# Hybrid attention trunk on one core: inverse norms of the queries as a row scale, head sums on column strips, memory keys and values in one product

## The chip, the cores and the metric

The kernel runs on one core of a Trainium2 chip. The metric is the device time of one execution in microseconds (us). Engines go by short names: PE is the matrix engine (TensorE), PEld its weight loads, DVE the vector engine, ACT the scalar engine, POOL the GpSimd engine, SP the engine that issues the weight loads from memory. A matmul here takes a stationary operand (K partitions by M columns) and streams N columns past it. A bank is one of PE's eight result buffers (128 partitions by 512 fp32 columns).

## The reference, cut to what matters

Two layers; 512 tokens, width 1024. The two SwiGLU parts and the output product are the same in both kernels. What the change touches is the mixing part between them:

```python
h = rms_norm(x, mix_norm[l]); z = h @ w_in[l]
aq, ak, av, iq, ik, iw, pu, mq = jnp.split(z, IN_OFFSETS, axis=-1)
aq = rms_norm(aq.reshape(B, S, 8, 64), q_norm[l])      # per head: a / rms(a) * gain
ak = rms_norm(ak.reshape(B, S, 8, 64), k_norm[l])
y_attn = dsa_attention(aq, ak, av, iq, ik, iw)         # top 128 keys by an indexer, softmax(q.k / 8) v
y_pool = multiscale_pool(pu, w_pool[l], pool_scale[l])
mk, mv = split(rms_norm(mem, mem_norm[l]) @ w_mem_kv[l])   # 256 memory tokens, 4 heads x 64
y_mem = softmax(rms_norm(mq) . rms_norm(mk) / 8) mv
x = x + concat(y_attn, y_pool, y_mem) @ w_out[l]
```

A row of logits is a query's dot products with all keys. 1/rms of the query is one number for the whole row, and the gain of the query can as well be multiplied into the keys.

## The kernel before, in words

Everything is written out by hand: each engine has its own program, and semaphores (`wait_ge`, `then_inc`) order them. A layer is `ffn`, `mix`, `ffn`. Activations lie transposed, channels on partitions, tokens on columns, as tiles of 128x512. Every fp32 product is made of three passes on rounded halves (hi.hi, hi.lo, lo.hi), so one product of a 128x128 weight block with a tile is three matmuls of 512 columns.

**Weights** come as a stream of slots of 512 KB (8 blocks of 128x128) through a ring of four. For a slot, SP loads `raw`; ACT (`round_ahead`, L911) waits until PE has finished the slot four places back, writes the rounded `w_hi` and the negated `w_lo`; POOL (`rest`, L380 on) issues a DMA that adds `raw` into `w_lo`; then PE may start the slot. In `mix` the slots are, in this order, iq 2, ik, iw, av 4, aq 4, ak 4, mq 2, pu 2, mk 2, mv 2, out 8.

**mix, projections.** `project_z` (L660) multiplies one slot with all of h into bank t % 4: 24 matmuls of 512 columns. DVE multiplies it by 1/rms of the tokens (`evacuate`, L1184) into a tile z, ACT squares it (`squares`, L1000) into one of two buffers, and PE sums the squares of each head (`heads_sum`, L584): one unrounded fp32 matmul a tile, 20 columns of selector against 512 tokens, all accumulated on rows 0 to 19 of bank 6. After the tenth tile ACT takes the root, DVE the reciprocal (`head_inverse`), and two small steps split it in hi and lo. Between the evacuations DVE takes the top eight scores of each token over and over (`take_largest`, L1228): 16 rounds a layer.

**mix, spreads and memory.** PE brings each head's inverse rms back to the head's 64 channel rows (`spread_rms`, L690: two matmuls with K = 20 into a bank), for all 4 query tiles, 4 key tiles, 2 memory query tiles and 2 memory key tiles, in `NORM_ORDER`; DVE multiplies the tile by it and the gain (`normalise`), ACT rounds it (`split_hi`), POOL makes the rest (L434). Between the spreads PE makes the memory keys (slots mk, 256 columns a matmul, channels on partitions) and the memory values (slots mv, tokens on partitions, 256 columns). Eight spreads stand ahead of the first logits, four behind.

**mix, attention.** 48 units: query tile 3 first, of each tile 8 heads and 4 memory heads. PE makes logits of two units at a time on the two row halves (`logits`, L781) in three banks in turn; DVE adds the mask, scales by -1/8 and takes the row's maximum (`mask_and_max`, L1310 on); ACT the exponential; PE transposes it (L806), DVE or ACT copies it, PE multiplies with the values on the two column halves (`times_v`, L810). Then the output product.

Of the kernel before, what the change touches and what calls it, by code (L numbers as in the profile page):

```python
# [21 lines left out]
P = 128  # L22
D = 1024
T = 512
LAYERS = 2
HD = 64
# [17 lines left out]
MIX_SLOTS = (("iq", 2), ("ik", 1), ("iw", 1), ("av", 4), ("aq", 4), ("ak", 4), ("mq", 2), ("pu", 2),  # L44
             ("mk", 2), ("mv", 2), ("out", 8))
# [12 lines left out]
G_Q, G_K, G_MQ, G_MK, G_POOL = (4 * DC + i for i in range(5))  # L58
# [3 lines left out]
ZT = HEADS // 2 * 2 + MEM_HEADS // 2  # L62
NORMED = ZT + MEM_HEADS // 2

Z_ROWS = 2 * ZT
MK_ROW = 32
MK_ROWS = 2 * (NORMED - ZT)
NROW = MK_ROW + MK_ROWS
# [4 lines left out]
C_SEL_MK = C_SEL + ZT * Z_ROWS  # L73
C_INV = C_SEL_MK + (NORMED - ZT) * MK_ROWS
# [8 lines left out]
ROUNDS_AT = (1, 1, 1, 1, 1, 1, 2, 2, 2, 2)  # L83
FIRST_ROUNDS = ROUNDS - sum(ROUNDS_AT)
# [14 lines left out]
ORDER = [0, 1, 2, 3, 4, 5, 6, 7, 8, 9, "mk"]  # L99

NORM_ORDER = [0, 4, 1, 5, 2, 6, 3, 7, 8, 9, 10, 11]
NORM_EARLY = 8

POOL_CHAIN = 14
ROUND_CHAIN = 2 * (TT - 1)
DVE_CHAIN = 104


def build(nc, x_t, mem_t, weights, pool_w, params, consts, spreads, out):
# [13 lines left out]
    def new(name, cols, dt=f32, parts=P):  # L123
# [4 lines left out]
    x = new("x", DC * T)  # L128
    h_hi = new("h_hi", DC * T, f32r)
# [16 lines left out]
    spread = new("spread", NORMED * P, f32r, NROW)  # L146
# [9 lines left out]
    wb = place("wb", T, a_lo_at + 11 * tile_b)  # L156
# [5 lines left out]
    hrms = place("hrms", T, a_lo_at, parts=NROW)  # L162
    hr_hi, hr_lo = (a_lo[0:NROW, i * T:(i + 1) * T] for i in (6, 7))
    spread_in = place("spread_in", NORMED * P, a_hi_at + 4 * tile_b, parts=NROW)
    v = place("v", TT * T, a_lo_at + 12 * tile_b)
    mk = place("mk", 2 * MEM, a_lo_at + 16 * tile_b)
    mv = place("mv", MT * MEM, a_lo_at + 17 * tile_b)
# [3 lines left out]
    rmem = place("rmem", MEM, small)  # L171
    negmax, rowsum, rinv = (
        place(name, UNITS, small + (MEM + i * UNITS) * 4)
        for i, name in enumerate(("negmax", "rowsum", "rinv")))
    top8 = place("top8", 8 * TT, small + (MEM + 3 * UNITS) * 4)
    sq = place("sq", DC * T, a_lo_at + 14 * tile_b)

    zn_hi = [h_hi[:, j * T:(j + 1) * T] for j in range(8)] + \
            [a_hi[:, j * T:(j + 1) * T] for j in (8, 9)] + \
            [a_hi[:, 10 * T + i * MEM:10 * T + (i + 1) * MEM] for i in range(2)]  # L180
    zn_lo = [h_lo[:, j * T:(j + 1) * T] for j in range(8)] + \
            [a_lo[:, j * T:(j + 1) * T] for j in (8, 9)] + \
            [a_lo[:, 10 * T + i * MEM:10 * T + (i + 1) * MEM] for i in range(2)]

    pt = [place(f"pt{i}", T, a_hi_at + (12 + j) * tile_b) for i, j in enumerate((0, 4, 6, 7))]

    prob = [t1[:, 0:T], t1[:, T:2 * T]] + \
           [place(f"prob{j}", T, a_hi_at + (12 + j) * tile_b)[:, :] for j in (1, 5)]


    rt = place("rt", T, a_hi_at + (12 + 2) * tile_b)
    yt = place("yt", T, a_hi_at + (12 + 3) * tile_b)
# [51 lines left out]
    mcols_done = sem("mcols_done")  # L244
    mcols_ready = sem("mcols_ready")
    v_ready = sem("v_ready")
    mv_ready = sem("mv_ready")
# [10 lines left out]
    spread_loaded = sem("spread_loaded")  # L258
# [49 lines left out]
    def spread_bank(k):  # L308

        return bank[k % 3 if k < NORM_EARLY else (7, 6)[k % 2]]  # L310

# [27 lines left out]
    def head_rms(j):  # L339

        return (slice(0, Z_ROWS), T) if j < ZT else (slice(MK_ROW, NROW), MEM)

    with nc.Block() as block:
# [32 lines left out]
        def _(pool):  # L376
# [15 lines left out]

            def pooling(l):

                wait_apart(pool, proj_ready, l * 17 + 16)
                for i in range(2):
                    ui = chunk(u, i)

# [25 lines left out]
            with pool.Fori(0, LAYERS) as l:  # L424
                with pool.Fori(0, ahead // RING) as i:
                    for pos in range(RING):
                        rest(l, (i * RING, pos))
# [1061 lines left out]
```

## Time and profile before

| | |
|---|---|
| median of 3 runs | 1983.04 us |
| lowest | 1982.92 us |
| the profiled execution, first to last instruction | 1981.4 us |
| PE busy | 1948.7 us (98%) |
| granted PE clock, mean | 0.996 of 2.4 GHz |
| sum of all waits of PE matmuls that the profile puts down to another engine or a DMA | 29.0 us |

The profile has no run time for the profiled execution other than its span; the median of the runs lies 1.6 us above it. Times in the trace count from the start of the span. The mixing part of the first layer runs from about 377 to 639 us, that of the second 979.8 us later. A busy PE is not one at its peak: the start of each matmul to the start of the next tells what it costs, since their ends overlap.

### The profile page before, as it was taken

The page shows a single profiled execution, that of the slowest core. Times are in us where ns is not written, and L with a number is a line of the kernel's source. Part 1 is how long each engine was busy: PE and PEld are TensorE (multiplying, and loading weights), DVE is VectorE, ACT ScalarE, POOL GpSimd, SP SyncE. Part 2 cuts the span into 40 slices and gives each one's busy share as a digit, 9 for nine tenths or more (in the row PEclk, how much of TensorE's full clock was granted, in tenths as well). Part 3 has the DMA queues.
Part 4 walks back from the last instruction along what each step waited for, and adds up shares of the span by engine and source line. Part 5 has one row for each costly group of instructions (what it writes and reads, how often), then busy time and mean ns, then how long its engine had stood idle before and what let it go on. Part 6 is the DMA issues. An engine that isn't in the chain of part 4 may idle for free.

```text
span 1981.4 us, 27709 instructions
## 1 busy us (share of the span) xinstructions
PE 1948.7 (98%) x9256; PEld 1571.9 (79%) x9256; DVE 617.1 (31%) x1180; ACT 1086.5 (55%) x1393; POOL 350.7 (18%) x404
## 2 busy tenths in 40 slices
PE   6999999999999999999999999999999999999999
PEld 4888888886768888888878888888767688888887
DVE  3222200367662322220052222004676532222101
ACT  6655543563584655553375565336546666565432
POOL 1111111111431111111111111111116111111111
PEclk9999999999999999999999999999999999999999
DMA  7988888887336888888878888888762379888886
GB/s 217 218 188 192 195 190 194 190 192 176 83 87 144 195 188 190 193 194 194 195 170 200 189 186 199 196 195 200 185 155 54 87 170 206 194 197 189 195 195 180
DMA packets 97799, 354.54 MB, mean 179 GB/s; under 512 B 11000, under 2 KB 11256, under 8 KB 97472
## 3 DMA queue, kind: packets, MB, share of 16 engines
q0 software_dynamic: 47232, 171.99, 48.7%
q1 hardware_dynamic: 49824, 178.84, 27.5%
q10 hardware_dynamic: 672, 2.80, 0.4%
q8 instruction: 40, 0.66, 0.1%
q14 instruction: 31, 0.25, 0.1%
HBM read 179.52 MB, written 2.10 MB: 92 GB/s over the span
## 4 chain that ended last, share of the span: by engine, by line
PE 97%; DMA 1%; ACT 1%; issue 1%; DVE 0%; SPq 0%; DVEq 0%; ACTq 0%; POOLq 0%
PE bank L453 95%; PE bank L806 2%; DMA w_lo<-raw 1%; DMA x<-x_t 0%; ACT w_lo L920 0%; ACT prob L1066 0%; DVE pt L336 0%; ACT a_hi L1082 0%; ACT t L1066 0%; DVE t L1323 0%; DVE x L1150 0%; DVE z L1277 0%; ACT pt L1059 0%; ACT mv L1046 0%; DVE yt L1341 0%
## 5 line engine op out<-in xcount | busy, mean ns | idle before, releaser
L919 ACT ACTIVATE w_hi<-raw 128x1024 fp32r<-128x1024 f32 x329 | 349.0, 1061 | 645.5 <-PE bank L453 630.8
L453 PE MATMUL bank<-h_hi,w_hi 128*128 128x512 f32 x1664 | 654.6, 393 | 15.9 <-ACT h_hi L891 13.9
L453 PE MATMUL bank<-h_hi,w_lo 128*128 128x512 f32 x1664 | 649.5, 390 | 5.6 <-DMA w_lo<-raw 5.6
L453 PE MATMUL bank<-h_lo,w_hi 128*128 128x512 f32 x1664 | 632.9, 389 | 0.0
L385 POOL DMA_DIRECT2D w_lo<-raw x328 | 283.5, 866 | 1589.6 <-ACT w_lo L920 1549.7
L453 PEld LDWEIGHTS bank<-h_hi,w_hi 128*128 128x128 f32 x1664 | 313.3, 188 | 97.5 <-ACT h_hi L891 15.3
L453 PEld LDWEIGHTS bank<-h_hi,w_lo 128*128 128x128 f32 x1664 | 313.3, 188 | 71.3 <-DMA w_lo<-raw 6.1
L453 PEld LDWEIGHTS bank<-h_lo,w_hi 128*128 128x128 f32 x1664 | 312.4, 188 | 65.5 <-issue 1.2
L920 ACT ACTIVATE w_lo<-raw 128x1024 fp32r<-128x1024 f32 x329 | 343.5, 1044 | 0.0
L453 PE MATMUL bank<-a_hi,w_hi 128*128 (+2 forms) x864 | 334.1, 387 | 0.0
L453 PE MATMUL bank<-a_lo,w_hi 128*128 (+2 forms) x864 | 332.8, 385 | 0.0
L453 PE MATMUL bank<-a_hi,w_lo 128*128 (+2 forms) x864 | 332.7, 385 | 0.0
L1150 DVE SCALAR_TENSOR_TENSOR x<-bank,x 128x512 f32<-128x512 f32 x48 | 32.7, 692 | 512.8 <-PE bank L453 512.8
L453 PEld LDWEIGHTS bank<-a_hi,w_hi 128*128 128x128 f32 x864 | 162.2, 188 | 35.0 <-issue 2.8
L453 PEld LDWEIGHTS bank<-a_hi,w_lo 128*128 128x128 f32 x864 | 162.3, 188 | 32.7
L453 PEld LDWEIGHTS bank<-a_lo,w_hi 128*128 128x128 f32 x864 | 162.3, 188 | 32.0
L1168 DVE TENSOR_TENSOR t<-bank,r 128x512 f32<-128x512 f32 x88 | 60.8, 691 | 384.2 <-PE bank L453 384.2
L919 ACT ACT_TABLE_LOAD x45 | 57.7, 1283 | 129.0 <-PE bank L453 121.1
L1165 DVE TENSOR_TENSOR t<-bank,r 128x512 f32<-128x512 f32 x88 | 60.9, 692 | 165.3 <-PE bank L453 163.6
L1174 DVE TENSOR_TENSOR a_lo<-t,a_hi 128x512 f32 x88 | 61.0, 693 | 107.8 <-ACT a_hi L938 107.8
L1172 DVE TENSOR_TENSOR t<-t,t 128x512 f32<-128x512 f32 x88 | 60.9, 692 | 11.1 <-ACT t L935 0.8
L935 ACT ACT_TABLE_LOAD x44 | 56.5, 1283 | 0.8
(138 smaller groups left out, 1273.9 us busy)
## 6 DMA issues: line engine op xcount, KB each, us to landing
raw<-weights SPq DMA_DIRECT2D x332, 512.0 KB, 4.6
w_lo<-raw POOLq DMA_DIRECT2D x328, 512.0 KB, 5.7
x<-x_t SPq DMA_DIRECT2D x4, 512.0 KB, 7.3
mem<-mem_t ACTq DMA_DIRECT2D x2, 1024.0 KB, 7.1
out_t<-x SPq DMA_DIRECT2D x8, 256.0 KB, 2.1
const<-consts SPq DMA_DIRECT2D x1, 505.5 KB, 10.1
spread_in<-spreads ACTq DMA_DIRECT2D x2, 216.0 KB
wpool<-pool_w ACTq DMA_DIRECT2D x2, 128.0 KB, 7.0
```

The lines of the kernel that those rows point to most:

```text
L385: G.dma_start(w_lo[:, s], raw[:, s], accum_op=ALU.add).then_inc(w_ready[pos], 16)
L453: return nc.tensor.matmul(out_, lhsT, rhs, start=start, stop=stop, skip_group_check=True)
L806: last = nc.tensor.transpose(bank[2 + n % 2][:, b * P:(b + 1) * P], prob[n % 4][:, b * P:(b + 1) * P], con(C_ID, P))
L919: nc.scalar.activation(w_hi[:, s], raw[:, s], ACT.Copy).then_inc(w_hi_done, 1)
L920: nc.scalar.activation(w_lo[:, s], raw[:, s], ACT.Copy, scale=-1.0)\
L935: nc.scalar.activation(g, g, ACT.Silu).then_inc(silu_ready, 1)
L1150: V.scalar_tensor_tensor(out=chunk(x, j), in0=bank[j][:, :], scalar=scale, in1=chunk(x, j), op0=ALU.mult, op1=ALU.add)\
L1165: V.tensor_tensor(out=g, in0=bank[2 * half][:, :], in1=r[:, :], op=ALU.mult).then_inc(gate_ready, 1)
L1168: V.tensor_tensor(out=h, in0=bank[2 * half + 1][:, :], in1=r[:, :], op=ALU.mult).then_inc(gu_free, 1)
L1172: V.tensor_tensor(out=h, in0=g, in1=h, op=ALU.mult).then_inc(prod_ready, 1)
L1174: V.tensor_tensor(out=a_lo[:, ds(f * T + half * T, T)], in0=h, in1=a_hi[:, ds(f * T + half * T, T)].bitcast(f32), op=ALU.subtract).then_in ...
```

## The change

1. **Queries.** Query tiles are no longer normalised. They are split in hi and lo as soon as they are evacuated (hi on ACT behind `square`, lo on POOL between the weight steps). The product of both gains, `gain_qk`, goes on the keys. The roots of the queries' sums are transposed by PE (`root_columns`), so that tokens lie on partitions, DVE inverts them with the factor -1/8 into `rq`, and `mask_and_max` takes `rq`'s column as its scale where it had a constant.
2. **Head sums.** `heads_sum(g)` handles four tiles in one group: four fp32 matmuls with 32 columns of selector each, whose results lie on the four 32-row strips of bank 6. Three groups (queries, keys, memory queries) take the place of ten sums of tiles.
3. **Key spreads.** Heads' inverse rms of the four key tiles lie on four 32-row strips; eight matmuls with K = 32 (four tiles, hi and lo) into banks 4 to 7 stand in one group. No other spreads are left.
4. **Memory keys and values.** One product with tokens on partitions: 4 slots kv, 48 matmuls of 512 columns, moved between ak and mq. ACT scales both by 1/rms of the memory tokens, DVE makes the heads' sums, inverses and normalised keys with tokens on partitions, PE transposes them (4 transposes).
5. The rounds of `take_largest` are dealt out anew (2 first, 10 between the tiles, 4 late), the tiles of the attention part move to the place of h, and the matrix of spreads is no longer loaded from memory.

```diff
-MIX_SLOTS = (("iq", 2), ("ik", 1), ("iw", 1), ("av", 4), ("aq", 4), ("ak", 4), ("mq", 2), ("pu", 2),
-             ("mk", 2), ("mv", 2), ("out", 8))
+MIX_SLOTS = (("iq", 2), ("ik", 1), ("iw", 1), ("av", 4), ("aq", 4), ("ak", 4), ("kv", 4), ("mq", 2),
+             ("pu", 2), ("out", 8))
-ROUNDS_AT = (1, 1, 1, 1, 1, 1, 2, 2, 2, 2)
-FIRST_ROUNDS = ROUNDS - sum(ROUNDS_AT)
+ROUNDS_AT = (1, 2, 1, 1, 1, 2, 1, 1)
+LATE_ROUNDS = 4
+FIRST_ROUNDS = ROUNDS - sum(ROUNDS_AT) - LATE_ROUNDS
...
@@ PE
-                def heads_sum(j):
-                    pe.wait_ge(zsq_ready, l * (ZT + 1) + (j + 1))
...
-                        last = mm(bank[6][0:Z_ROWS, :], con(C_SEL + ORDER[j] * Z_ROWS, Z_ROWS),
-                                  chunk(t1, j % 2), j == 0, j == ZT - 1)
+                def heads_sum(g):
+                    pe.wait_ge(zsq_ready, l * ZT + (QT, 2 * QT, ZT)[g])
...
+                    for s in range(QT):
+                        last = mm(bank[6][s * STRIP:(s + 1) * STRIP, :], con(C_SEL, STRIP),
+                                  squares[s % MQT if g == 2 else s])
                     last.then_inc(zsum_done, 1)
+                def root_columns(g):
+                    pe.wait_ge(hrms_ready, l * ROOT_GROUPS + (g + 1))
+                    if g == 2:
+                        pe.wait_ge(zn_ready, (l + 1) * QT)
+                    for i in range(TT):
+                        last = nc.tensor.transpose(bank[7][:, i * P:(i + 1) * P],
+                                                   hrms[g][:, i * P:(i + 1) * P], con(C_ID, P))
+                    last.then_inc(rq_done, 1)
...
+                def project_kv(s):
+                    n = at("kv", s)
+                    lo_ready_of(l, n)
+                    for half in range(2):
+                        k = 2 * s + half
+                        for i in range(MT):
+                            last = passes(bank[4 + i][:, :], pair(m_hi, m_lo, k * MEM + i * P, P),
+                                          weight(n % RING, half * T, T), k == 0, k == DC - 1)
+                    last.then_inc(slot_done, 1)
                 for i in range(4):
                     project_z(4 + i, "aq", i)
...
+                project_z(8, "ak", 0)
+                heads_sum(0)
+                project_z(9, "ak", 1)
+                project_z(10, "ak", 2)
+                root_columns(0)
+                project_z(11, "ak", 3)
+                pe.wait_ge(m_lo_ready, l + 1)
+                project_kv(0)
+                project_kv(1)
+                heads_sum(1)
+                project_kv(2)
+                project_kv(3)
                 project_z(12, "mq", 0)
+                pe.wait_ge(spread_ready, l + 1)
+                pe.wait_ge(hr_lo_ready, l + 1)
+                pe.wait_ge(kv_ready, (l + 1) * MT)
...
+                for part, hr in enumerate((hr_hi, hr_lo)):
+                    for s in range(QT):
+                        rows = slice(s * STRIP, (s + 1) * STRIP)
+                        last = mm(bank[4 + s][:, :], spread[rows, :], hr[rows, :], part == 0, part == 1)
...
                 project_z(13, "mq", 1)
+                pe.wait_ge(mk_n_ready, l + 1)
+                pe.wait_ge(zn_ready, l * QT + 1)
+                for c in range(MQT):
+                    for i in range(MT):
+                        last = nc.tensor.transpose(bank[4][:, c * MEM + i * P:c * MEM + (i + 1) * P],
+                                                   mk_n[:, i * MEM + c * P:i * MEM + (c + 1) * P],
+                                                   con(C_ID, P))
+                last.then_inc(mkt_done, 1)
                 project_z(14, "pu", 0)
+                heads_sum(2)
                 project_z(15, "pu", 1)
+                root_columns(2)
...
@@ ACT
+                for j in range(QT):
                     round_ahead(l, MIX_BASE["aq"] + j)
+                    square(j)
+                    split_hi(j)
+                for j in range(QT):
+                    round_ahead(l, MIX_BASE["ak"] + j)
+                    if j == 0:
+                        head_root(0)
+                    square(QT + j)
+                round_ahead(l, MIX_BASE["kv"])
+                round_ahead(l, MIX_BASE["kv"] + 1)
                 head_root(1)
+                round_ahead(l, MIX_BASE["kv"] + 2)
+                act.wait_ge(hinv_ready, l + 1)
+                nc.scalar.activation(hr_hi, hrms[1][:, :], ACT.Copy).then_inc(hr_hi_ready, 1)
+                round_ahead(l, MIX_BASE["kv"] + 3)
+                act.wait_ge(rmem_ready, l + 1)
                 for i in range(MT):
+                    nc.scalar.activation(chunk(kv, i), bank[4 + i][:, :], ACT.Copy,
+                                         scale=rmem_col[:, i:i + 1]).then_inc(kv_ready, 1)
...
@@ DVE, from the eighth tile on
+                for j in range(2 * QT):
+                    evacuate_z(j)
+                    rounds(ROUNDS_AT[j])
+                inverse_columns(0)
+                dve.wait_ge(hrms_ready, l * ROOT_GROUPS + 2)
+                V.reciprocal(hrms[1][:, :], hrms[1][:, :]).then_inc(hinv_ready, 1)
+                rounds(1)
+                dve.wait_ge(hr_hi_ready, l + 1)
+                V.tensor_tensor(out=hr_lo, in0=hrms[1][:, :], in1=hr_hi.bitcast(f32),
+                                op=ALU.subtract).then_inc(hr_lo_ready, 1)
+                dve.wait_ge(kv_ready, (l + 1) * MT)
...
+                V.tensor_reduce(mk_rms[:, :], mk_sq[:, :].rearrange("p (g d) -> p g d", d=HD),
+                                mybir.AxisListType.X, ALU.add).then_inc(mk_sum_ready, 1)
+                rounds(1)
+                evacuate_z(2 * QT)
...
-                                           scale=-HD ** -0.5, scalar=-TAKEN, op0=ALU.add, op1=ALU.min,
+                                           scale=unit_rq(n), scalar=-TAKEN, op0=ALU.add, op1=ALU.min,
```

On PE, behind the last projection of the kernel before (slot pu 1): a spread's matmul reads `a_lo` (where the inverse rms lie) and `spread`; matmuls on `a_hi`/`a_lo` with `w_` of 256 columns are the memory keys.

```order
L453 MATMUL bank<-h_hi,w_lo 128x512
L696 REGISTER_ALU
L698 REGISTER_ALU
L453 MATMUL bank<-a_lo,spread 128x512 x2
...
L453 MATMUL bank<-a_hi,w_hi 128x256
L453 MATMUL bank<-a_lo,w_hi 128x256
L453 MATMUL bank<-a_hi,w_lo 128x256
```

The same engine in the changed kernel, behind the slot mq 0 and behind the slot mq 1:

```order
L472 MATMUL bank<-h_hi,w_lo 128x512
L728 REGISTER_ALU
L730 REGISTER_ALU
L472 MATMUL bank<-a_hi,spread 128x512 x8
L695 REGISTER_ALU
...
L741 ISA
L744 MATMUL bank<-const,mk_n 128x128 x4
```

All spreads stand in one piece now, with a projection behind it, and the memory keys reach PE again only as four transposes, behind one more projection.

On DVE, ahead of the first mask of the kernel before (names: `score` is the mask, `hrms` the inverse rms of the heads):

```order
L1277 SCALAR_TENSOR_TENSOR z<-z,par,bank 128x512 x4
L1290 REGISTER_ALU
L1293 TENSOR_TENSOR mk<-bank,rmem 128x256 x2
L1277 SCALAR_TENSOR_TENSOR z<-z,par,bank 128x512 x3
L1261 REGISTER_ALU
L1262 RECIPROCAL hrms<-hrms 4x256
L1267 TENSOR_TENSOR a_lo<-hrms,a_lo 4x256
L320 ISA
L1323 ISA t_59,negmax<-bank,score 128x512
```

On DVE in the changed kernel, from the split of the keys' inverse rms to the normalised memory keys:

```order
L1299 TENSOR_TENSOR a_hi<-hrms_k,a_hi 128x512
L1303 REGISTER_ALU
L1305 TENSOR_TENSOR mk_sq<-kv 128x512
L1139 REGISTER_ALU
L1307 TENSOR_REDUCE mk_rms<-mk_sq 128x8
...
L1206 TENSOR_TENSOR z<-bank,r 128x512
L1313 ISA
L1315 SCALAR_TENSOR_TENSOR z<-z,gain_qk,bank 128x512
...
L1318 RECIPROCAL mk_rms<-mk_rms 128x8
L1139 REGISTER_ALU
L1321 TENSOR_TENSOR mk_n<-kv,mk_rms 128x256 x2
```

Between the reduction and the evacuation of `z` stands one round of `take_largest` (three MAX, three MATCH_REPLACE). The twelve multiplications of tiles by spread inverses have become four, and a chain of memory keys stands among them.

## Rows read from the trace of the kernel before

**Rows 1.** The page, busy time of each engine.

```profile
PE 1948.7 (98%) x9256; PEld 1571.9 (79%) x9256; DVE 617.1 (31%) x1180; ACT 1086.5 (55%) x1393; POOL 350.7 (18%) x404
```

**Rows 2.** PE, timeline, projections of the first layer (start us, us, engine, line, operation, idle before).

```profile
404.69 0.39 PE L453 MATMUL bank<-w_hi,h_hi 128*128 128x512 f32 x1
...
415.35 0.39 PE L453 MATMUL bank<-w_hi,h_lo 128*128 128x512 f32 x1
...
477.70 0.50 PE L453 MATMUL bank<-h_hi,w_hi 128*128 128x512 f32 x1
...
483.37 1.03 PE L453 MATMUL bank<-t,const 128*20 128x512 f32 x2
484.34 0.60 PE L453 MATMUL bank<-const,rmem 1*128 1x1 f32 x4
...
503.82 1.89 PE L453 MATMUL bank<-t,const 128*20 128x512 f32 x4
```

**Rows 3.** PE, timeline, spreads and memory products, first layer.

```profile
511.47 1.18 PE L453 MATMUL bank<-a_lo,spread 20*128 20x512 f32 x4
...
512.80 0.28 PE L453 MATMUL bank<-a_lo,w_hi 128*128 128x256 f32 x1
...
515.43 0.28 PE L453 MATMUL bank<-a_hi,w_lo 128*128 128x256 f32 x1
...
529.15 0.50 PE L453 MATMUL bank<-h_hi 64*128 64x512 f32 x2
```

**Rows 4.** The chain that ended last (start us, us, what), second layer and first.

```profile
1491.31 17.76 PE bank L453 x116
549.03 0.59 PE bank L806 x4
```

**Rows 5.** PE, timeline, unrounded products with the values on column halves.

```profile
540.98 1.09 PE L453 MATMUL bank<-pt,v 128*64 128x128 f32 x16
542.01 0.39 PE L453 MATMUL bank<-a_hi 64*128 64x256 f32 x2
```

**Rows 6.** PE, timeline, the first logits.

```profile
531.77 0.50 PE L453 MATMUL bank<-h_hi 64*128 64x512 f32 x2 [0.54 <-DVE negmax L1323]
532.11 0.40 PE L453 MATMUL bank<-h_lo,h_hi 64*128 64x512 f32 x2
532.34 0.39 PE L453 MATMUL bank<-h_hi,h_lo 64*128 64x512 f32 x2
...
534.42 0.79 PE L453 MATMUL bank<-h_hi 64*128 64x512 f32 x2
```

**Rows 7.** Stretches of the attention's start: us, busy of each engine, granted clock, DMA share, GB/s.

```profile
534.00:540.00 6.00, 6.00 (x25) 3.96 (x25) 4.01 (x12) 4.45 (x12) 5.79 (x10) 0.50 0.01 1
```

**Rows 8.** DVE, timeline, a round of the top eight, a reciprocal, the first mask.

```profile
497.90 1.47 DVE L1236 MAX8 top<-score 128x8 f32<-128x512 f32 x3
...
500.86 1.47 DVE L1236 MAX8 top<-score 128x8 f32<-128x512 f32 x3
...
506.61 3.34 DVE L1262 RECIPROCAL hrms<-hrms 20x512 f32<-20x512 f32 x1 [1.99 <-ACT hrms L1018]
...
531.02 0.69 DVE L1323 CUSTOM_DVE_ANT_0 t<-bank,score 128x512 f32<-128x512 f32 x1
```

**Rows 9.** ACT, timeline, rounding of one slot.

```profile
504.00 1.06 ACT L919 ACTIVATE w_hi<-raw 128x1024 fp32r<-128x1024 f32 x1 [4.18 <-PE bank L453]
504.97 1.04 ACT L920 ACTIVATE w_lo<-raw 128x1024 fp32r<-128x1024 f32 x1
```

**Rows 10.** The page, DMA queues and issues (KB each, us to landing).

```profile
q0 software_dynamic: 47232, 171.99, 48.7%
q1 hardware_dynamic: 49824, 178.84, 27.5%
...
raw<-weights SPq DMA_DIRECT2D x332, 512.0 KB, 4.6
w_lo<-raw POOLq DMA_DIRECT2D x328, 512.0 KB, 5.7
```

More of the change, by code:

```diff
@@ L57 @@
 G_FFN1, G_MIX, G_FFN2, G_MEM = 0, DC, 2 * DC, 3 * DC
-G_Q, G_K, G_MQ, G_MK, G_POOL = (4 * DC + i for i in range(5))
+G_Q, G_MQ, G_K, G_MK, G_POOL = (4 * DC + i for i in range(5))
 PARAMS = 4 * DC + 4 + 2
[L62 to L68, printed above, removed]
+QT = HEADS // 2
+MQT = MEM_HEADS // 2
+ZT = 2 * QT + MQT
+STRIP = 32
+PROJ = 3 + 1 + ZT + 2
+ROOT_GROUPS = 3
 C_ID = 0
@@ new lines, in mix @@
+                square(2 * QT)
+                for j in range(QT, 2 * QT):
+                    act.wait_ge(zn_ready, l * QT + (j - QT + 1))
+                    act.wait_ge(zlo_ready, l * ZT + (j - QT + 1))
+                    split_hi(j)
+                square(2 * QT + 1)
+                split_hi(2 * QT)
+                split_hi(2 * QT + 1)
+                act.wait_ge(mkt_done, l + 1)
+                act.wait_ge(gain_ready, l + 1)
+                nc.scalar.activation(zmk_hi, bank[4][:, :], ACT.Copy,
+                                     scale=gain_qk[:, 1:2]).then_inc(mk_hi_ready, 1)
@@ L1252, in mix, with rounds @@
+                def rounds(n):
+                    for _ in range(n):
                         take_largest(l * DVE_CHAIN + links[0])
                         links[0] += ROUND_CHAIN
[L1254 to L1262 removed]
@@ new lines, in mix @@
+                evacuate_z(2 * QT)
+                dve.wait_ge(gain_ready, l + 1)
+                for s in range(QT):
+                    dve.wait_ge(spread_done, l * QT + (s + 1))
+                    t = chunk(z, QT + s)
+                    V.scalar_tensor_tensor(out=t, in0=t, scalar=gain_qk[:, 0:1], in1=bank[4 + s][:, :],
+                                           op0=ALU.mult, op1=ALU.mult).then_inc(zn_ready, 1)
+                dve.wait_ge(mk_rms_ready, l + 1)
+                link(l, V.reciprocal(mk_rms[:, :], mk_rms[:, :]))
@@ new lines, in mix @@
+                for i in range(MT):
+                    s = slice(i * MEM_HEADS, (i + 1) * MEM_HEADS)
+                    last = V.tensor_tensor(
+                        out=mk_n[:, i * MEM:(i + 1) * MEM].rearrange("p (h d) -> p h d", d=HD),
+                        in0=kv[:, i * T:i * T + MEM].rearrange("p (h d) -> p h d", d=HD),
+                        in1=mk_rms[:, s].unsqueeze(2).broadcast_to([P, MEM_HEADS, HD]), op=ALU.mult)
+                last.then_inc(mk_n_ready, 1)
+                rounds(1)
@@ L1402, in _constants @@
     c[:, C_EPS] = EPS
-    return c
-def _spread():
-    import numpy as np
-    c = np.zeros((NROW, NORMED * P), np.float32)
-    for head in range(2 * NORMED):
-        row = head if head < Z_ROWS else MK_ROW + head - Z_ROWS
-        c[row, head * HD:(head + 1) * HD] = 1
     return c
```

364 lines of the change are left out of this document (142 added, 222 removed).

## The prediction

> **What bounds the kernel now.** I read the page first: PE is busy for 1948.7 us of a span of 1981.4 [rows 1], so a change pays what it takes from PE's own stream and from the few places where PE stands. Since the ends of matmuls overlap, I price them by the distance between starts, in the timeline of PE. The unrounded sums and the spreads stand in the mixing part alone, so I read one layer's and count it twice: the last piece ahead of the attention is 17.76 us long in the second layer [rows 4], as from 511.47 to 529.15 in the first [rows 3].
>
> Prices of one step: 48 matmuls of 512 columns in sequence start 10.66 us apart, first to last, so 0.227 us each [rows 2]. A projection with a head sum behind it takes 6.64 us (477.70 to 484.34), and 24 x 0.227 is 5.45: a sum costs 1.20. Two sums at once show 1.89 against 1.03 us: the second adds 0.86. So 0.86 is the unrounded matmul of 512 columns itself, and 0.34 the change of shape there and back [rows 2]. Of 256 columns, 23 matmuls start 2.63 us apart, first to last, 0.120 each [rows 3]: two of them cost 0.24, where one of 512 columns costs 0.227. Four transposes cost 0.59 [rows 4].
>
> Rows 6 and 7 show where PE stands: between the first logits (529.15) and the third pair (534.42) it waits for DVE's masks and spreads, and the granted clock is 0.50, which is 1.2 GHz, from 534 to 540.
>
> **What the change removes, for one layer.** Ten head sums: eight alone and one pair, 8 x 1.20 + 2.06 = 11.7 us. The columns of the memory's rms: 0.5 (start of the row to the next projection) [rows 2]. The whole piece from 511.47 to 529.15 with eight spreads, memory keys, memory values and the keys' sum: 17.7 [rows 3]. Together 29.9. Twelve projections of tiles stay. The mean square of the memory stays one short step.
>
> **What it adds, for one layer.** Memory keys and values: 48 x 0.227 = 10.9. Two transpositions of the roots and one of the memory keys: 3 x (0.59 + 0.2 for the change of shape, of which 0 to 0.34 is possible) = 2.4.
>
> The three groups of sums are the disputed term. If the four strips run at the same time, a group costs what one sum does, 1.2. If they run in pairs, 2 x 0.86 + 0.34 = 2.1. If they run one behind the other, 4 x 0.86 + 0.34 = 3.8. No row shows four strips. Two column halves do run together: eight unrounded products of 128 columns should take 8 x 0.86/4 = 1.7 us one by one, and take 1.03 with the change of shape [rows 5]. That is so close to full overlap that I take 1.4 for a group of four, just above full overlap and below pairs; three groups are 4.2, between 3.6 and 11.4. The Trainium skill, TensorE: Matmul & The Clock Gate, section Measured speedup vs the span model, gives 2.38 times for three column strips and 3.07 times for four row strips; an estimate by 3.07 is 4 x 0.86/3.07 + 0.34 = 1.46 a group, 4.4 for three, which would move the forecast by 0.4 us. No run here shows it yet.
>
> Spreads: eight rounded matmuls with K = 32 on four row strips. Two row halves overlap fully: the pair at 532.11 is followed by the next 0.23 us later, which is the price of one matmul [rows 6]. All four at once would be 2 x 0.227 + 0.34 = 0.8, one by one 8 x 0.227 + 0.34 = 2.1; I take 0.9.
>
> **Waits.** With T for the end of the fourth key projection, PE runs kv 0 and 1 (5.5), a group of sums (1.4), kv 2 and 3 (5.5), mq 0 (5.5), and reaches the spreads at T+17.9 and the memory keys' transposes at T+24.2. The chain on ACT and DVE: ACT roots the keys' sums at T+8.4, behind rounding a slot (1.9 us a slot, [rows 9]); DVE's reciprocal takes 3.34 [rows 8], so T+11.8; ACT rounds the first half of it, then waits in `round_ahead(kv 3)` for the raw slot. That load may start only when the slot's `w_lo` has landed: T + 2.3 for ACT + 5.7 + 4.6 [rows 10] = T+12.6, some 2 us later if the short slots crowd the queues. So ACT scales kv by T+15.8 to T+17.5: no wait at the spreads. Queued behind that on DVE are square and reduction (1.6 with the wait between), one round of the top eight (2.96, [rows 8]), the evacuation of mq 0 (0.69, as the mask's row of 512 columns), four key tiles (2.8), and memory keys (1.1): T+25 to T+26.7 against T+24.2. PE waits there 0.9 to 2.6 us; I take 1.8, with 0 to 3.5 as bounds. Behind PE's wait stand pu 0, the last sums and pu 1, and nothing else is late for them. Ahead of the first logits PE now waits for the evacuation of pu 1, partly under the transposes: 0.3.
>
> The sum added is 10.9 + 2.4 + 4.2 + 0.9 + 1.8 + 0.3 = 20.5, and 29.9 - 20.5 = 9.4 saved.
>
> **The weight stream.** A kv slot keeps PE for 12 x 0.227 = 2.7 us where others keep it 5.4. A slot is ready 2.3 (ACT) + 5.7 (landing) = 8.0 us after the slot four places back is done. For kv 3 three short slots and a sum stand between, 9.6 us: slack 1.6. For mq 0 it is alike. Before, the four memory slots were drawn out over 17.7 us. In engine time a slot costs 0.487 x 1981/328 = 2.9 us for the addition and 0.275 x 1981/332 = 1.6 for the load [rows 10], 4.6 against 2.7. I take no wait, with up to 3 us a layer as the far bound.
>
> **The start of the attention.** The 5.27 us from the first to the third pair hold four spreads, four multiplications on DVE and the late memory inverse: the first mask starts at 531.02, about 0.9 us after its logits, since DVE was splitting it [rows 8]. Without these, a pair of logits takes 0.8 to 0.9, the mask may start 0.25 behind, and the pairs come 2.0 us apart: 4.1, which saves 1.2 (0 to 2). ACT and POOL shed four tiles each there. The half clock stays: PE still stands about 1.1 us twice, as much as before. The scale of the mask read from memory instead of a constant I cost at nothing: the row's 0.69 us for 512 columns is one column per step, with the mask read beside it. ACT's earlier splits (0.6 each, four) lie in its waits for PE, 4 us a slot [rows 9]; POOL's lie between its slots. If it cost 0.1 us more, the three pairs at the start would carry 0.2 each, 0.6 a layer.
>
> So a layer saves 9.4 + 1.2 = 10.6 us, both 21.2; the profiled span would be 1960.2, and the median, 1.6 above, 1961.8.
>
> **The rivals.**
> - **PE keeps its full clock** at the attention's start. The six microseconds from 534 to 540 are all busy at half clock [rows 7], so up to 3.0 is lost; with it back, 2 x 3.0 less: 1955.8. For it: the spreads that waited are gone. Against it: PE still stands for masks. The rule of the Trainium skill (TensorE: Matmul & The Clock Gate, section HAM oscillation) asks for long idle gaps before a fall; the gap here was 0.54 us [rows 6], twice, so the trace does not bear it out, and I keep the fall.
> - **Strips do not overlap.** Groups 3.8, spreads 2.1: 7.2 + 1.2 = 8.4 more a layer, 1978.6. Against it speaks [rows 5].
> - **Slower than before: each strip pays the change of shape.** If PE drains between strips, a strip's sum costs the 1.20 of a sum of today, twelve of them 14.4 instead of 4.2, and eight spreads 8 x 0.57 = 4.5 instead of 0.9: 13.8 more a layer, 1989.4. It turns slower once a group of sums costs over 1.4 + 10.6/3 = 4.9 us. Against it: eight products on halves in 1.03 us [rows 5] leave no room for a drain between them.
> - **The weights come late.** The short slots crowd the queues, PE stands 3 us for kv 3 or mq 0, and the clock falls once more (3.0): 6.0 a layer, 1973.8. It decides from a landing over 7.3 us.
>
> **How the numbers follow.** The forecast holds 0.70, with a range of its own of 1955 to 1969: waits 0 to 3.5 instead of 1.8 (-4 to +3), groups 1.2 to 2.1 (-1 to +4), the start 0 to 2 (-2 to +2). Full clock 0.12, late weights 0.08, strips in sequence 0.07, drains 0.03. The range of 1951 to 1975 leaves out the two last and edges of the others. A change of 2% is about what a measurement of this kernel can tell from no change: faster than 1943.4 needs a saving of 20 us a layer, which only the full clock together with every lower bound comes near, 0.02; slower than 2022.7 is 0.01; the rest 0.97.
>
> **What would show it.** Each group of sums adds 1.2 to 1.6 us between two projections, the eight spreads under 1.0; the piece from the memory's mean square to the first logits is 9 to 10 us shorter; PE stands at the transposes of `mk_n` for a release by DVE; the first three pairs of logits stand 2 us apart; the clock is half for some 6 us behind them. I am wrong if a wait for `w_lo` shows inside kv, if a group takes over 2.1, or if the attention itself, from the third pair to the output product, changes its length by more than 2 us, since I let nothing of it count.

## The result and the profile after

| | before | after |
|---|---|---|
| median | 1982.98 us (4 runs) | 1968.45 us (4 runs) |
| the profiled execution | 1981.4 us | 1965.5 us |
| PE matmuls | 9256 | 9148 |
| PE busy | 1948.7 us | 1918.9 us |

One of the four runs before took 2177.24 us, far slower than the three others, and is left out of the ratio. The ratio of the times is 0.993, with a 95% interval of 0.9918 to 0.9942: faster by 0.7%, well within the 2% that count as no change. The forecast was 1961.8 us, its range 1951 to 1975.

The page of the changed kernel, busy time, then the issues (the lines that answer to [rows 1, 10]):

```profile
PE 1918.9 (98%) x9148; PEld 1559.4 (79%) x9148; DVE 614.1 (31%) x1176; ACT 1082.7 (55%) x1391; POOL 347.6 (18%) x400
...
raw<-weights SPq DMA_DIRECT2D x332, 512.0 KB, 4.7
w_lo<-raw POOLq DMA_DIRECT2D x328, 512.0 KB, 5.8
```

PE shed 29.8 us of busy time, yet the span only 15.9. The other half must stand somewhere as idle time. PE's waits in the changed kernel (what it waited for: us in total, times, longest):

```profile
PE bank L744 <- DVE mk_n L1321: 8.5, 2, 4.3
PE bank L472 <- DMA w_lo<-raw: 7.7, 2, 5.7
PE bank L472 <- DVE negmax L1364: 4.3, 4, 1.1
...
PE bank L472 <- ACT kv L1049: 1.5, 1, 1.5
```

The line of `mk_n` is new and the largest wait that the change brought: twice 4.3 us at the transposes of the memory keys. PE's timeline there and at the spreads, first layer (start, us, engine, line, operation, idle before):

```profile
497.88 0.74 PE L472 MATMUL bank<-a_hi,spread 32*128 32x512 f32 x8 [1.53 <-ACT kv L1049]
498.55 0.50 PE L472 MATMUL bank<-h_hi,w_hi 128*128 128x512 f32 x1
...
508.55 0.65 PE L744 MATMUL bank<-const,mk_n 128*128 128x128 f32 x4 [4.26 <-DVE mk_n L1321]
508.96 0.61 PE L472 MATMUL bank<-h_hi,w_hi 128*128 128x512 f32 x1
...
512.34 0.50 PE L472 MATMUL bank<-h_hi,w_lo 128*128 128x512 f32 x1
```

From 508.96 to 512.34 eight matmuls take 3.38 us where they take 1.8 elsewhere (8 x 0.227). The stretches say why: behind the wait the clock is granted at half. Stretches of both places (us, busy of each engine, granted clock, DMA share, GB/s):

```profile
509.00:510.00 1.00, 1.00 (x5) 0.81 (x4) 1.00 (x5) 0.00 (x0) 0.55 (x1) 0.58 0.00 0
510.00:511.00 1.00, 1.00 (x3) 0.79 (x3) 1.00 (x5) 0.00 (x0) 0.00 (x0) 0.50 0.00 0
...
525.00:533.00 8.00, 5.98 (x52) 4.10 (x52) 7.00 (x20) 6.49 (x17) 7.34 (x10) 1.00 0.01 3
```

At the start of the attention, where [rows 7] had half clock, it now stays full (last line).

The chain that ended last, which here led through PE before [rows 4], now leaves it. Read it downwards: each piece was released by the one above (start, us, what):

```profile
479.81 1.05 ACT w_lo L932
...
481.42 6.17 DMA w_lo<-raw
487.75 6.48 DMA raw<-weights
...
494.59 1.06 ACT w_hi L931
...
496.60 1.16 ACT kv L1049 x2
497.78 0.70 DVE mk_sq L1305
...
502.75 2.63 DVE z L1315 x4
...
506.94 1.49 DVE mk_n L1321
508.55 0.65 PE bank L744 x4
```

So the memory keys wait for a weight load that they don't use: ACT stands in `round_ahead` for the raw slot of pu 1 (landed at 494.2) and only then scales kv. Behind that comes DVE's queue.

The head sums, first layer, and the two parts of kv around the second group:

```profile
460.72 1.06 PE L472 MATMUL bank<-t,const 128*32 128x512 f32 x8
461.72 0.50 PE L472 MATMUL bank<-h_hi,w_hi 128*128 128x512 f32 x1
...
478.64 0.39 PE L472 MATMUL bank<-w_hi,a_hi 128*128 128x512 f32 x1
...
484.17 1.06 PE L472 MATMUL bank<-t,const 128*32 128x512 f32 x8
485.17 0.50 PE L472 MATMUL bank<-w_hi,a_hi 128*128 128x512 f32 x1
...
490.75 0.39 PE L472 MATMUL bank<-h_hi,w_hi 128*128 128x512 f32 x1
```

A group of four sums costs 1.2 with the change of shape, what one sum cost before [rows 2]. The 24 matmuls from 478.64 take 5.5, as priced.

The first logits, which answer to [rows 6]: three pairs 2.0 us apart, 523.80 to 527.88, 4.08 us in place of 5.27, with a wait of 1.1 for a mask ahead of the second and of the third.

```profile
523.80 0.72 PE L472 MATMUL bank<-a_hi 64*128 64x512 f32 x4 [0.43 <-DVE u L1206]
...
525.85 0.73 PE L472 MATMUL bank<-a_hi 64*128 64x512 f32 x4 [1.09 <-DVE negmax L1364]
...
527.88 0.73 PE L472 MATMUL bank<-a_hi 64*128 64x512 f32 x4 [1.07 <-DVE negmax L1364]
...
531.91 1.09 PE L472 MATMUL bank<-pt,v 128*64 128x128 f32 x16
```

**The ledger**, by marks that both kernels have (us, before and after):

| stretch of the mixing part | layer 1 | saved | layer 2 | saved |
|---|---|---|---|---|
| first index logits to first logits | 101.67 / 96.67 | 5.00 | 101.67 / 96.02 | 5.65 |
| first logits to first product with the values | 11.83 / 8.11 | 3.72 | 11.72 / 8.11 | 3.61 |
| from there to the last product with memory values | 57.06 / 57.42 | -0.36 | 57.07 / 57.41 | -0.34 |
| sum | | 8.36 | | 8.92 |

With 0.35 us that it was ahead already at the first mark, and 1.7 that it loses at the start of the second layer, these are the 15.9 us. That loss goes with a fall of the clock behind the wait for the first weights of the second layer (0.81, 0.50 and 0.83 in the three stretches of 2 us from 996). The kernel before has the same wait of 2.0 us there, and no fall.

### The profile page after: what moved, and what is told of

Same layout as the page of the kernel before. It is cut to its first block, busy times and chain, and to the rows that moved or that the text cites. A ratio compares the mean times of both kernels' runs of the same rounds, so it can differ in the third digit from the quotient of the medians.

```text
span 1965.5 us, 27449 instructions
## 1 busy us (share of the span) xinstructions
PE 1918.9 (98%) x9148; PEld 1559.4 (79%) x9148; DVE 614.1 (31%) x1176; ACT 1082.7 (55%) x1391; POOL 347.6 (18%) x400
## 4 chain that ended last, share of the span: by engine, by line
PE 94%; DMA 2%; DVE 1%; issue 1%; ACT 1%; DVEq 0%; SPq 0%; ACTq 0%; POOLq 0%
PE bank L472 92%; PE bank L821 1%; DMA w_lo<-raw 1%; DMA raw<-weights 1%; ACT w_lo L932 0%; DMA x<-x_t 0%; DVE z L1315 0%; DVE mk_n L1321 0%; ACT prob L1086 0%; DVE t L1364 0%; ACT kv L1049 0%; ACT t L1086 0%; ACT w_hi L931 0%; DVE pt L344 0%; PE bank L744 0%
## 5 line engine op out<-in xcount | busy, mean ns | idle before, releaser
L472 PE MATMUL bank<-h_hi,w_hi 128*128 128x512 f32 x1664 | 656.0, 394 | 15.6 <-ACT h_hi L903 13.6
L472 PE MATMUL bank<-a_hi,w_hi 128*128 (+1 forms) x832 | 324.6, 390 | 0.0
L472 PE MATMUL bank<-a_lo,w_hi 128*128 (+1 forms) x832 | 323.8, 389 | 0.0
L472 PE MATMUL bank<-a_hi,w_lo 128*128 (+1 forms) x832 | 323.7, 389 | 0.0
L472 PEld LDWEIGHTS bank<-a_hi,w_hi 128*128 128x128 f32 x832 | 156.2, 188 | 33.7 <-issue 1.4
L472 PEld LDWEIGHTS bank<-a_hi,w_lo 128*128 128x128 f32 x832 | 156.2, 188 | 32.5
L472 PEld LDWEIGHTS bank<-a_lo,w_hi 128*128 128x128 f32 x832 | 156.2, 188 | 32.0
```

Source lines behind the costliest of these rows:

```text
L472: return nc.tensor.matmul(out_, lhsT, rhs, start=start, stop=stop, skip_group_check=True)
```

## The experiments

**1 to 3. The wait at the memory keys.** Two causes stood to be told apart: ACT scales kv late, behind the load for pu 1; and DVE comes to `mk_n` late, behind four key tiles, where its two multiplications ran 1.44 us each. The changed kernel's DVE and POOL there show that they ran at the same time as POOL's subtractions:

```profile
504.24 5.31 POOL L440 TENSOR_TENSOR a_hi<-z,a_hi 128x512 fp32r<-128x512 f32 x4 [6.21 <-ACT a_hi L1019]
...
505.53 2.88 DVE L1321 TENSOR_TENSOR mk_n<-kv,mk_rms 128x256 f32<-128x256 f32 x2
```

`kv_first`: ACT scales kv ahead of rounding the slot of pu 1.

```diff
-                round_ahead(l, MIX_BASE["kv"] + 3)
+                act.wait_ge(slot_done, l * SLOTS + (RING + MIX_BASE["kv"] + 4))
                 act.wait_ge(rmem_ready, l + 1)
                 for i in range(MT):
                     nc.scalar.activation(chunk(kv, i), ...).then_inc(kv_ready, 1)
+                round_ahead(l, MIX_BASE["kv"] + 3)
```

> The changed kernel with one swap on ACT: the memory keys and values are scaled before the slot pu 1 is rounded, so that they no longer stand behind its raw load. Theory 1 (the late load starts the DVE chain late): kv is ready at about 492 instead of 497.8 us, the 1.5 us wait at the spreads goes, the wait at the transposes of mk_n falls from 4.3 to about 2.1 us a layer; some 3 us a layer less, about 1962 us. Theory 2 (DVE's own queue, with the rounds of the top eight, sets when mk_n is ready): the wait stays at 4.3 us and the time at 1968 us.

Measured: 1960.34 us, ratio 0.9885 (0.9869 to 0.9902), span 1958.3. The wait at the spreads is gone, that at `mk_n` falls from 8.5 to 2.8 in two. The two multiplications start at 502.88 and still take 2.97 together.

`mkn_early`: DVE makes the memory keys ahead of the evacuation of mq 0 and of the four key tiles.

```diff
+                dve.wait_ge(mk_rms_ready, l + 1)
+                link(l, V.reciprocal(mk_rms[:, :], mk_rms[:, :]))
...
+                last.then_inc(mk_n_ready, 1)
                 evacuate_z(2 * QT)
                 dve.wait_ge(gain_ready, l + 1)
                 for s in range(QT):
...
-                dve.wait_ge(mk_rms_ready, l + 1)
-                link(l, V.reciprocal(mk_rms[:, :], mk_rms[:, :]))
...
-                last.then_inc(mk_n_ready, 1)
```

> The changed kernel with the reciprocal and the two multiplications of mk_n on DVE moved ahead of the evacuation of mq 0 and the four key tiles; everything else as it is. They then run while POOL does nothing. Theory 1 (each took 1.44 us because POOL's subtractions ran beside them): each takes 0.42 to 0.5 us, PE's wait of 4.3 us at the transposes falls to 0 to 0.5, the half clock behind it goes as well: 4 to 6 us a layer less, about 1957 us. Theory 2 (the operand that is spread over 64 columns costs it): each still takes about 1.4 us, wherever it stands; the wait falls only to 1.5 to 2.5 us, about 1962 us.

Measured: 1959.09 us, ratio 0.9879 (0.9862 to 0.9895), span 1957.2. No wait at `mk_n` is left, and the two multiplications take 0.76 together, with POOL idle until 505.56 but for a DMA issue:

```profile
502.71 0.76 DVE L1314 TENSOR_TENSOR mk_n<-kv,mk_rms 128x256 f32<-128x256 f32 x2
```

So the same instruction starts every 0.4 us alone and 1.4 us beside POOL's subtractions. The wait for kv at the spreads stays (2.6 in two, 2.3 of it in the first layer, where the clock falls behind it: 0.79 from 496 to 504).

`both`: the two edits together.

> Both moves together. If the 4.3 us and the 1.5 us are the late load and the place of mk_n, no wait at the spreads or at the transposes is left, the clock stays full through the projections, and the time is 1952 to 1956 us. If the clock falls by itself (at the attention's start instead, as in the kernel before), 3 us a layer come back and the time is near 1960 us.

Measured: 1954.8 us, ratio 0.9873 (0.9852 to 0.9895), span 1952.7. Neither wait is left, 10.0 us of idle time less. Each edit alone takes away most of the wait at `mk_n` or all of it, so what they gain doesn't add up: 7.2 and 8.3 us of span alone, 12.8 together. Of the 12.8, 10.0 are these waits; the rest goes with the clock, whose falls behind the wait at `mk_n` are gone, while one at the attention's start has come. The clock is full through the first layer's mixing part, but falls at the second layer's start, and at the attention's start in that layer:

```profile
518.00:524.00 6.00, 4.68 (x33) 3.11 (x34) 4.98 (x16) 5.17 (x14) 5.60 (x8) 1.00 0.02 4
1484.00:1492.00 8.00, 6.95 (x34) 4.51 (x32) 5.00 (x16) 4.92 (x14) 7.41 (x10) 0.57 0.01 3
```

**4 and 5. Do the strips overlap?** A group at 1.2 us says so, but a low price of each strip would look alike. `twice` (on the changed kernel) issues every group of sums and the spreads twice over; `one_strip` (on `both`) adds four sums to each group as well, all four on the first strip. Both add matmuls whose results are overwritten.

The added lines of `twice` (the first of them for the sums), then of `one_strip`:

```diff
+                    for s in range(QT):
+                        mm(bank[6][s * STRIP:(s + 1) * STRIP, :], con(C_SEL, STRIP), squares[...])
...
+                for part, hr in enumerate((hr_hi, hr_lo)):
+                    for s in range(QT):
+                        mm(bank[4 + s][:, :], spread[rows, :], hr[rows, :], part == 0, part == 1)
```

```diff
+                    for s in range(QT):
+                        mm(bank[6][0:STRIP, :], con(C_SEL, STRIP), squares[...])
```

> The changed kernel with each group of four head sums and the group of eight spreads issued twice; the second issue overwrites the first with the same values. Theory 1 (four strips run at the same time): a second group of sums adds 0.86 us, a second group of spreads 0.45 us: 3.0 us a layer. Rival (strips in pairs): 1.7 and 0.9 us. Rival (one by one): 3.4 and 1.8 us, 12 us a layer.

> Both moves, and ahead of each group of four head sums four more sums, all on the first strip; the group then overwrites them. Theory 1 (what made the second group cost 0.86 us is that its strips differ): four on one strip run one by one, 3.4 us a group, 10.3 us a layer. Rival (a narrow sum is cheap by itself, whatever strip it takes): 0.9 us a group as in the doubled kernel.

The first group in `twice`, with its spreads, then in `one_strip`:

```profile
460.38 1.92 PE L472 MATMUL bank<-t,const 128*32 128x512 f32 x16
...
500.29 1.22 PE L472 MATMUL bank<-a_hi,spread 32*128 32x512 f32 x16 [2.27 <-ACT kv L1056]
```

```profile
459.96 4.48 PE L472 MATMUL bank<-t,const 128*32 128x512 f32 x16
```

Measured, one run each: 1972.95 and 1973.14 us. Four more sums on four strips add 0.86 us (1.92 for 1.06), the price of a single unrounded matmul of 512 columns; four more on one strip add 3.42, four times that. The eight extra spreads add 0.48 (1.22 for 0.74), which is two matmuls' time for eight. No run puts all eight on one row strip, but the kernel before has spreads on one strip, six and then four in a row, all on the first 20 rows:

```profile
515.64 1.65 PE L453 MATMUL bank<-a_lo,spread 20*128 20x512 f32 x6
...
520.29 1.19 PE L453 MATMUL bank<-a_lo,spread 20*128 20x512 f32 x4
```

There two matmuls more add 0.46, so few rows alone don't make them cheap. Strips overlap fully, column strips as row strips.

**6. The scale from memory.** The prediction let the row's own scale cost nothing. In the changed kernel a mask takes 0.75 us, in [rows 8] 0.69. `const_scale` puts the constant back, on `both`; it leaves out the queries' inverse rms.

```diff
-                                           scale=unit_rq(n), scalar=-TAKEN, ...
+                                           scale=-HD ** -0.5, scalar=-TAKEN, ...
```

> Both moves, and the mask on DVE scales by the constant -1/8 as in the kernel before; the queries' norm is left out of the result. Theory 1 (the scale read per row costs the mask 0.06 us of 512 columns, and that is what the attention lost between the first product with the values and the output product, 0.35 us a layer): masks at 0.69 instead of 0.75 us, the stretch shorter by 0.3 to 0.4 us a layer, the time about 1954 us. Theory 2 (the mask is hidden): masks shorter, the stretch as long as before.

Measured: 1952.27 us, ratio 0.9842 (0.9822 to 0.9862), span 1949.9. The masks of DVE in `both`, then in `const_scale`:

```profile
517.26 0.75 DVE L1363 CUSTOM_DVE_ANT_0 t<-bank,score,rq 128x512 f32<-128x512 f32 x1 [1.29 <-PE bank L472]
```

```profile
516.84 0.69 DVE L1363 CUSTOM_DVE_ANT_0 t<-bank,score 128x512 f32<-128x512 f32 x1 [1.29 <-PE bank L472]
```

0.06 us a mask, and at the attention's start, where PE stands for masks, the three pairs come 1.98 apart instead of 2.05. From the first product with the values to the last with memory values the first layer takes 57.20 instead of 57.44. So the scale costs some 0.1 at the start and 0.24 behind it, a part of the ledger's third line. The rest of its 2.8 us of span is mostly the clock, which did not fall at the attention's start in the second layer here (1.00 from 1481 to 1489); that the shorter mask did that is not shown, since it stays full in the next run too, with the mask at 0.75. The intervals of `both` and of this run overlap.

**7. Wide or narrow.** How much of the gain is the width of kv's matmuls? `narrow_kv` takes `both` and makes kv of 96 matmuls of 256 columns. The two column halves of a bank are accumulated in turns, which changes what memory keys and values hold; its time stands for the matmuls alone.

```diff
-                            last = passes(bank[4 + i][:, :], pair(...), weight(n % RING, half * T, T), ...)
+                            for c in range(0, T, MEM):
+                                last = passes(bank[4 + i][:, c:c + MEM], pair(...),
+                                              weight(n % RING, half * T + c, MEM), ...)
```

> Both moves, and the memory product in 96 matmuls of 256 columns instead of 48 of 512, with the same slots and place. Theory 1 (a matmul of 256 columns starts every 0.120 us, one of 512 every 0.227): the four slots take 11.5 instead of 10.9 us of matmuls, 0.6 us a layer more. Rival (the gain of one product is the saved weight loads, hidden only at 512 columns): 2 us a layer or more.

PE's timeline, the first matmuls of kv and the first behind it:

```profile
479.93 0.28 PE L472 MATMUL bank<-w_hi,a_hi 128*128 128x256 f32 x1
480.05 0.28 PE L472 MATMUL bank<-w_lo,a_hi 128*128 128x256 f32 x1
...
492.63 0.40 PE L472 MATMUL bank<-h_hi,w_hi 128*128 128x512 f32 x1
```

Measured, one run: 1955.9 us. From 479.93 to 492.63 are 12.70 us for kv with a group of sums, where the changed kernel takes 12.11 (478.64 to 490.75). The width is worth 0.6 us a layer, 0.24 against 0.227 for 512 columns as priced. It is no large part of the gain.

**8 and 9. The gaps at the first logits.** In `both` PE still stands 1.1 us for each of two masks, in both layers. `pu_in_gaps` fills them: the last pool projection is cut in two, and a half stands behind the first pair of logits and one behind the second (`root_columns(2)` goes with the first half).

```diff
-                project_z(15, "pu", 1)
-                root_columns(2)
...
                     if n < UNITS:
                         logits(n)
+                    if n < 4:
+                        project_pu1(n // 2)
```

> Both moves, and the last projection (pu 1) cut in two halves of 12 matmuls, one behind the first pair of logits and one behind the second; its evacuation on DVE stands behind the fourth mask, and ACT's third exponential waits for it. Theory 1 (PE's three waits at the attention's start, 0.4 + 1.1 + 1.1 us, are free room): 2.6 us a layer less than both moves alone, and no half clock at that place: 1947 to 1951 us. Theory 2 (the exponential and the mask that now wait set the start anew): the waits come back behind the third pair, the time stays at 1953 to 1956 us.

Measured: 1954.02 us, ratio 0.9853 (0.9834 to 0.9872), span 1951.6. The gaps are filled (0.7 us for masks in two waits, 4.3 before), but PE now stands once a layer ahead of the first logits. Its wait, then the stretch behind it in the first layer:

```profile
PE bank L472 <- DVE u L1222: 3.8, 2, 1.9
```

```profile
510.00:516.00 6.00, 5.41 (x20) 3.87 (x21) 1.89 (x5) 2.25 (x5) 0.00 (x0) 0.72 0.01 3
```

Pu 1 had been the cover of DVE's work on pu 0. Of the 3.6 us filled, 2.9 come back as this wait (3.8 against 0.9) and 0.7 at the copies of `pt` (2.8 against 2.1), and the clock falls twice here as in `both`, only behind other waits: no gain over `both` that can be told. DVE evacuates pu 0 behind the mask made of the scores and the memory keys' low part:

```profile
507.77 1.43 DVE L1348 TENSOR_SCALAR score<-score 128x1152 f32<-128x1152 f32 x1
509.13 0.74 DVE L1351 SCALAR_TENSOR_TENSOR a_lo<-bank,gain_qk,a_hi 128x512 fp32r<-128x512 f32 x1
509.79 0.68 DVE L1222 TENSOR_TENSOR u<-bank,r 128x512 f32<-128x512 f32 x1
```

`gaps_early_u` moves it ahead of both, and the mask made of the scores to the end, on top of `pu_in_gaps`:

```diff
+                evacuate(14, MIX_BASE["pu"], chunk(u, 0), bank[2][:, :], r[:, :])
-                V.tensor_scalar(score[:, :], score[:, :], TAKEN, NEG, ...).then_inc(bias_ready, 1)
                 V.scalar_tensor_tensor(out=zmk_lo, ...).then_inc(mk_lo_ready, 1)
-                evacuate(14, MIX_BASE["pu"], chunk(u, 0), bank[2][:, :], r[:, :])
+                V.tensor_scalar(score[:, :], score[:, :], TAKEN, NEG, ...).then_inc(bias_ready, 1)
```

> The kernel of the run before with pu 1 in two halves in the gaps of the first logits, and in it one step of DVE moved: the evacuation of the first pool tile stands behind the last rounds of the top eight and ahead of the rest of the memory keys and of the mask made from the scores, and these two change places. Theory 1, the wait of PE at the first logits (3.8 us in 2 places) is a place in DVE's queue and nothing else: the evacuation starts some 2 us earlier (at about 507.8 in place of 509.8), PE stands under 0.8 us there in place of 1.9, and the first mask starts behind the scores' mask. That gives about 1.2 us a layer, 2.4 in all, so a ratio of about 0.984 and a span of about 1949; if the granted clock no longer falls behind this wait, up to 2.5 us a layer more, 1944. Rival, the steps of DVE from the last round to the first mask are a chain of fixed length (0.7 + 0.7 + 1.4 + the mask): then PE is released earlier and stands as much longer at the third pair of logits for the first mask, the sum of its waits for DVE stays within 0.5 us of 4.5 + 2.8, and the span stays within 1 us of 1951.6.

Measured: 1949.86 us, ratio 0.9832 (0.9819 to 0.9846), span 1947.7. PE's wait in that place, and a stretch of either layer:

```profile
PE bank L472 <- DVE a_lo L1349: 1.3, 2, 0.7
```

```profile
508.00:520.00 12.00, 11.34 (x60) 7.53 (x60) 6.27 (x17) 4.20 (x8) 1.89 (x2) 1.00 0.01 1
1474.00:1490.00 16.00, 15.58 (x114) 11.47 (x114) 9.95 (x28) 9.77 (x24) 6.44 (x9) 1.00 0.01 2
```

The wait falls from 1.9 to 0.7 us a layer and no new one takes its place: the first theory holds, the chain of fixed length doesn't. One detail came out otherwise: the evacuation starts at 509.82, no earlier than in the run before (509.79), since this profile runs 1.3 us later up to there (the evacuation ahead of it starts at 505.39 instead of 504.10) and DVE now waits 0.78 us for PE. What counts is its place against PE's own work: PE began to stand at 508.68 in the run before (logits at 510.60, less the wait of 1.92), 1.1 us ahead of the evacuation's start, and at 510.78 in this one (511.44 less 0.66), 1.0 behind it. The granted clock is full in the whole profile; the expectation had put a span of 1944 for that, and it is 1947.7. This is the fastest kernel of the study, 18.6 us below the changed one.

## Why the prediction was right, and where it was off

The measured 1968.45 us lies inside the range that the forecast had for itself, 1955 to 1969, but only just: 6.7 us above the forecast, of a change that saved 14.5.

**The strips** (right, a little better than taken). "I take 1.4 for a group": 1.2. Spreads at 0.9: 0.8. Transposes at 0.8 each: 0.5 to 0.6. Both rivals on strips are ruled out by `twice` and `one_strip`: a second group adds 0.86, which leaves no room for strips in sequence or for a drain between them. The estimate from the Trainium skill, TensorE: Matmul & The Clock Gate, section Measured speedup vs the span model (1.46 a group, by its factor of 3.07 for four row strips), is above what ran here: four strips cost what one does, a factor of 4.0 on columns (3.42 against 0.86) and about as much on rows.

**Removed work and kv** (right). The 5.5 us of two kv slots are there, and removing 29.9 and adding what was measured gives the ledger's first line: kv 10.9, three groups 3.6, spreads 0.8, transposes 1.8, the waits 4.3, 1.5 and 0.4, and the half clock 1.6 are 24.9, so 5.0 saved, as measured (5.00). That it comes out so closely is luck: the terms are rounded, and by distances of starts the first four transposes cost 0.46.

**The waits** are the step that failed, by their size: "PE waits there 0.9 to 2.6 us; I take 1.8, with 0 to 3.5 as bounds", and it was 4.26 in each layer, outside the bounds. "No wait at the spreads": 1.5 in one layer. Two terms carry this. The raw load of pu 1 landed 15.6 us behind T in the first layer (478.64 to 494.23), not 12.6 or some 2 later: the first of its two DMAs began 0.5 us later than taken, and they took 6.2 and 6.5 us instead of their medians of 5.7 and 4.6. That the short slots crowd the queues fits the DMA share (1.01 to 1.08 in stretches of 2 us from 484 to 494, 0.73 to 0.89 from 440 to 478), but no run tests it. And I priced the memory keys on DVE at 1.1 by DVE alone, where their multiplications ran 2.88 beside POOL. `kv_first` and `mkn_early` each took one of them away, `both` together, and the waits went.

**Weights** (right): no wait for `w_lo` inside kv. The crowded queue showed as ACT's wait for `raw` instead (3.7 us). The slack is small, though: `kv_first` has a wait of 0.41 inside kv, `both` one of 0.45 ahead of mq 0.

**The clock** (wrong in place; near in sum by luck). "The half clock stays": it did not; it went from the attention's start, which the rival at 0.12 had, and gave 2.5 us a layer (third pair of logits to the first product with the values 4.03 us against 6.56). But the clock fell behind the new wait at `mk_n` (1.6 us lost in the first layer, about 2.5 in the second), and at the second layer's start (1.7), which nothing in the prediction had. These cancel almost, so the forecast is nearer than its steps were.

**The signs that it named.** Three did not come as told. The stretch up to the first logits is 5.0 and 5.65 us shorter, not 9 to 10. The clock is not at half behind the first pairs. And the prediction called itself wrong if the attention, from the third pair to the output product, changes its length by more than 2 us: it is 2.2 us shorter in the first layer (6.56 to 4.03 us, less the 0.36 of the ledger's third line) and 2.1 in the second. What it let count for nothing there, the clock, counts.

**The attention's start and body.** 5.27 to 4.1: 4.08. The scale of the mask was put at nothing, and at 0.6 us a layer if a mask took 0.1 more: it takes 0.06 more, and with it the attention from its first product with the values is 0.35 longer. `const_scale` puts 0.24 of that to the scale.

**The sum.** Forecast 21.2 us of span, measured 15.9, so 5.3 short. The waits took 6.4 more than forecast (2 x 2.46 + 1.5), the clock 0.8 (1.6 + 2.5 + 1.7 lost, 2 x 2.5 gained), the attention's body 0.7; strips, spreads and transposes gave back 2.6 (2 x 1.3). That is 5.3; the 0.35 ahead at the first mark and the waits at the first logits, 0.1 longer than forecast, are left out. The median stands 1.3 us further from the forecast, since it lies 2.95 us above its span here and 1.6 in the kernel before; 0.9 of that is that the profiled run was the fastest of the four (1967.57).

## What to carry to other kernels

Small products that use 32 of 128 columns or rows belong in groups of four on their strips: each group cost what one did. When work leaves PE, list for every result that PE then waits for what stands ahead of it in the queues of the others, a load that it does not use among them; here the order of two steps on ACT and of two on DVE was worth 13 us, nearly as much as the whole change. A wait of one or two microseconds may cost as much again in clock behind it, so fill or remove it before counting instructions, and look whose cover the filling work was.

## What the runs showed of the hardware that I had not expected

- DVE's multiplication of 128x256 with two operands from memory starts every 0.4 us with POOL idle and every 1.4 us while POOL runs its own subtractions. The mask made of the scores (128x1152), which reads one tensor only, is slower there too: 0.68 us before, 1.43 beside POOL; 0.75 in `gaps_early_u`, where POOL had ended. An evacuation from a bank beside POOL's subtractions (505.39 in that run) took 0.68, as elsewhere. The Trainium skill has the rule (SBUF — State Buffer, section Who interferes with whom): a vector instruction with both inputs in SBUF and a GpSimd instruction that reads SBUF exclude each other for the whole of one. The rows agree in that each multiplication takes as long as a subtraction and a little more (1.44 against 1.27 alone). They don't show the reverse in full: POOL's four subtractions beside the two multiplications took 5.31 us, in `mkn_early` without them 5.06, so they lost 0.25 and not twice 0.4. Weighed beforehand, it would have put 2 us more on the wait at `mk_n`; the prediction did not draw on it.
- A scale read from memory per row adds 0.06 us to a mask of 512 columns.
- Where the clock falls is not to be read from the length of a wait alone. It fell behind waits of 4.3 us (`mk_n`) and 1.9 (`pu_in_gaps`) in both layers; at the attention's start two waits of 1.1 us brought a fall in both layers of `kv_first` and none in the changed kernel; in `both` they brought one in the second layer (0.57 from 1484 to 1492) and none in the first. At a wait of 0.45 us near 417, which all kernels here have, it fell in `kv_first` and `narrow_kv` (0.72 from 416 to 422) and in no other kernel. What decides it stays open, and so does the fall at the second layer's start behind a wait of some 2 us, which the kernel before, `twice`, `narrow_kv` and both kernels with pu 1 in the gaps don't show.
